# Heads of a gated DeltaNet: output norm as three columns through memory, triangular inverse handed on by tile in two PSUM banks

## The reference

```python
lmat = jnp.where(strict, jnp.einsum('nbhid,nbhjd->nbhij', k_beta, kb) * decay, 0.0)
sol = lax.linalg.triangular_solve(lmat + jnp.eye(c), rhs, left_side=True, lower=True, unit_diagonal=True)
...                                   # then a scan over chunks: v_new, o_c, state s
gate = jax.nn.silu(h @ w_g).reshape(bsz, t, GDN_HEADS, GDN_DV)
o = rmsnorm(o, o_norm_g) * gate       # o * rsqrt(mean(o*o over the 128 channels) + EPS) * g
return o.reshape(bsz, t, GDN_HEADS * GDN_DV) @ w_out, new_buf, s_new
```

## Time and profile before

| what | value |
|---|---|
| three runs, median | 1553.15 us (1552.4 to 1556.8) |
| the profiled execution | 1552.87 us, span 1551.2 us, granted clock 0.99 |
| TensorE busy | 1517.4 us, 98% of the span |
| VectorE, ScalarE, GpSimd busy | 52%, 47%, 70% |
| DMA | 212.47 MB, mean 137 GB/s |

### The profile page before, as it was taken

One profiled execution on the slowest core, in us unless ns is written; L12 is line 12 of the kernel. 1 busy time (PEld: TensorE's weight loads), 2 busy tenths in 40 slices (PEclk: granted clock), 3 DMA queues, 4 the chain that ended last, 5 costly groups with the idle time before them and its releaser, 6 DMA issues.

```text
span 1551.2 us, 32241 instructions
## 1 busy us (share of the span) xinstructions
PE 1517.4 (98%) x10218; PEld 1472.9 (95%) x10218; DVE 800.8 (52%) x1791; ACT 734.7 (47%) x1406; POOL 1081.6 (70%) x1040
## 2 busy tenths in 40 slices
PE   9999999999999999999999999999899999999998
PEld 8999999998999999888999999999888889999997
DVE  4555454017555413996655521576667776555401
ACT  6654444446444435556544433557544434443432
POOL 5568887774777678985867777666655656767674
PEclk9999999999999999999999999999999999999999
DMA  6334444552444655322565445544412225444353
GB/s 237 125 128 146 153 154 151 150 153 87 162 148 150 160 150 170 93 71 73 159 170 156 144 129 146 187 136 136 138 44 93 72 95 175 155 153 145 121 152 110
DMA packets 88109, 212.47 MB, mean 137 GB/s; under 512 B 25600, under 2 KB 33312, under 8 KB 88032
## 3 DMA queue, kind: packets, MB, share of 16 engines
q1 hardware_dynamic: 88032, 211.49, 42.7%
HBM read 201.80 MB, written 9.66 MB: 136 GB/s over the span
## 4 chain that ended last, share of the span: by engine, by line
PE 91%; DVE 5%; issue 1%; ACT 1%; POOL 1%; DMA 1%; DVEq 0%; SPq 0%; POOLq 0%; ACTq 0%
PE bank L887 26%; PE bank L889 26%; PE bank L888 26%; PE bank L1125 2%; PE bank L1264 1%; PE bank L1275 1%; PE bank L1319 1%; PE bank L1178 1%; POOL M L715 0%; DMA fst<-in_d_st 0%; DVE bank L2242 0%; PE bank L1349 0%; PE bank L1150 0%; DVE ssq L1934 0%; PE bank L1301 0%
## 5 line engine op out<-in xcount | busy, mean ns | idle before, releaser
L609 POOL TENSOR_TENSOR wlo<-raw,whi 128x512 fp32r<-128x512 f32 (+3 forms) x398 | 457.8, 1150 | 379.2 <-ACT whi L1412 341.5
L887 PE MATMUL bank<-Gh,whi 128*128 128x320 f32 x1912 | 596.4, 312 | 3.3 <-DVE M L2224 1.9
L889 PE MATMUL bank<-Gh,wlo 128*128 128x320 f32 x1912 | 590.9, 309 | 0.0
L888 PE MATMUL bank<-Gl,whi 128*128 128x320 f32 x1912 | 590.8, 309 | 0.0
L611 POOL TENSOR_TENSOR wlo<-raw,whi 128x512 fp32r<-128x512 f32 (+3 forms) x398 | 478.6, 1202 | 0.0
L1412 ACT ACTIVATE whi<-raw 128x1024 fp32r<-128x1024 f32 (+3 forms) x400 | 374.8, 954 | 51.5 <-PE bank L889 40.3
L887 PEld LDWEIGHTS bank<-Gh,whi 128*128 128x128 f32 x1912 | 359.0, 188 | 5.8 <-DVE M L2224 2.2
L888 PEld LDWEIGHTS bank<-Gl,whi 128*128 128x128 f32 x1912 | 359.0, 188 | 1.1
L889 PEld LDWEIGHTS bank<-Gh,wlo 128*128 128x128 f32 x1912 | 358.9, 188 | 0.0
L887 PE MATMUL bank<-Hh,whi 128*128 128x320 f32 x912 | 283.6, 311 | 4.0 <-DVE Hl L2183 2.5
L889 PE MATMUL bank<-Hh,wlo 128*128 128x320 f32 x912 | 281.8, 309 | 0.0
(11 more groups left out here) (389 smaller groups left out, 1807.1 us busy)
## 6 DMA issues: line engine op xcount, KB each, us to landing
raw<-in_f_up SPq DMA_DIRECT2D x176, 512.0 KB, 3.3
raw<-in_f_down SPq DMA_DIRECT2D x64, 384.0 KB, 3.1
raw<-in_f_down SPq DMA_DIRECT2D x64, 320.0 KB, 3.1
raw<-in_c_pw SPq DMA_DIRECT2D x24, 512.0 KB, 3.6
raw<-in_a_in SPq DMA_DIRECT2D x16, 512.0 KB, 4.2
raw<-in_d_qk SPq DMA_DIRECT2D x16, 512.0 KB, 3.6
raw<-in_d_vg SPq DMA_DIRECT2D x16, 512.0 KB, 3.5
raw<-in_a_out SPq DMA_DIRECT2D x8, 512.0 KB, 3.5
```

The lines of the kernel that those rows point to most:

```text
L609: pool.tensor_tensor(wlo[k][:, 0:half], raw[k][:, 0:half], whi[k][:, 0:half].bitcast(F32), ALU.subtract).then_inc(half_ready, 1)
L887: nc.tensor.matmul(dst, wh, h, start=start and n == 0, stop=False)
L888: nc.tensor.matmul(dst, wh, lo, start=False, stop=False)
L889: ins = nc.tensor.matmul(dst, wl, h, start=False, stop=stop and end and n == len(tiles) - 1)
```

## The change

It does two things. First, in levels 1 to 4 each product is written in two groups of tiles (`GROUPS`), each in its own bank, with a semaphore step per group: TensorE's product, ScalarE's copy and VectorE's subtraction of group 1 no longer wait for group 2. Level 0 stays one group of three; level 1 is split into tile 0 and tiles 1 and 2; levels 2 to 4 into two single tiles. The transposes still take a whole head. Second, the output norm's sums are three columns of 128 tokens (sq as the weight, one column of ones moving), ScalarE takes the root of the three columns of each head into `rinv`, VectorE takes one reciprocal of both heads' six columns at the start of the next pair, SyncE stores them to a DRAM row and loads the row back broadcast to all partitions into sq, and `head_scale` waits for that load. The decays of the queries (QT) move: head 0 before level 0, head 1 between level 0's subtractions and its transposes.

```diff
+        rinv = [dc[:, 2 + 3 * x:5 + 3 * x] for x in range(2)]
+        scr_r = nc.dram_tensor("scr_r", [HEADS, TW], F32).ap()
+        GROUPS = (((0, 3),), ((0, 1), (1, 3)), ((0, 1), (1, 2)), ((0, 1), (1, 2)), ((0, 1), (1, 2)))
+        COPIES, CHANGES = (2 * sum(len(g) for g in GROUPS[:n]) for n in (5, 4))
+        def group_at(lev, x):
+            return 2 * sum(len(g) for g in GROUPS[:lev]) + x * len(GROUPS[lev])
+        def below_bank(lev, g, x):
+            return bank[4 * x + (0, 1 if lev == 4 else 2)[g]]
+        def change_bank(g, x):
+            return bank[4 * x + (3, 1)[g]]
...
@@ SyncE @@
+            def gdn_norms(b):
+                sp.wait_ge(rinv_ready, b * 1 + 1)
+                for x in range(2):
...
+                        sp.dma_start(dst.rearrange("(i p) -> p i", p=P), rinv[x]).then_inc(norms_stored, 16)
+            def gdn_norm_loads(b):
+                sp.wait_ge(norms_stored, b * 32 + 32)
+                for x in range(2):
...
+                    sp.dma_start(sq[x][:, 0:NT], src.partition_broadcast(P)).then_inc(norms_in[x], 16)
...
                     with sp.Fori(1, 4) as b:
                         gdn_row_loads(b)
                         gdn_state_stores(b - 1)
+                        gdn_norms(b - 1)
                         gdn_state_loads(b)
+                        gdn_norm_loads(b - 1)
...
                     gdn_state_stores(3)
+                    gdn_norms(3)
+                    gdn_norm_loads(3)
...
@@ TensorE, below @@
-                        else:
-                            pe.wait_ge(tm_ready, b * 8 + (2 * (lev - 1) + x + 1))
+                        elif lev == 1:
+                            pe.wait_ge(kv_scaled, b * 2 + (x + 1))
                         pe.wait_ge(lv_ready, b * 10 + (2 * lev + x + 1))
-                        for c in range(3 if lev < 2 else 2):
-                            ins = nc.tensor.matmul(T(bank[4 * x], c), T(LV[x][lev], c), T(Tm[x], c), start=True, stop=True)
-                        ins.then_inc(lt_done, 1)
+                        for g, (a, z) in enumerate(GROUPS[lev]):
+                            if lev == 1:
+                                pe.wait_ge(tm_ready, b * CHANGES + (x + 1))
+                            elif lev > 1:
+                                pe.wait_ge(tm_ready, b * CHANGES + (group_at(lev - 1, x) + g + 1))
+                            for c in range(a, z):
+                                ins = nc.tensor.matmul(T(below_bank(lev, g, x), c), T(LV[x][lev], c), T(Tm[x], c),
+                                                       start=True, stop=True)
+                            ins.then_inc(lt_done, 1)
...
@@ TensorE, change @@
-                        pe.wait_ge(b_ready, b * 10 + (2 * lev + x + 1))
...
+                        if lev == 1:
+                            pe.wait_ge(qt_ready, b * 2 + (x + 1))
+                        for g, (a, z) in enumerate(GROUPS[lev]):
+                            pe.wait_ge(b_ready, b * COPIES + (group_at(lev, x) + g + 1))
+                            for c in range(a, z):
+                                ins = nc.tensor.matmul(T(change_bank(g, x), c), T(TT[x], c), T(Bm[x], c), start=True, stop=True)
+                            ins.then_inc(bt_done, 1)
...
@@ TensorE, last_change_turned @@
                         for c in range(2):
-                            ins = nc.tensor.matmul(T(bank[4 * x + 2], c), T(Bm[x], c), T(TT[x], c), start=True, stop=True)
-                        ins.then_inc(tb_done, 1)
+                            pe.wait_ge(b_ready, b * COPIES + (group_at(4, x) + c + 1))
+                            nc.tensor.matmul(T(bank[4 * x + 2 + c], c), T(Bm[x], c), T(TT[x], c), start=True, stop=True)\
+                                .then_inc(tb_done, 1)
...
@@ TensorE, sums of the output norm @@
-                        nc.tensor.matmul(bank[4 * x + 2][:, 0:NT], ones[:, :], sq[x][:, 0:NT], start=True, stop=True)\
-                            .then_inc(osum_done, 1)
+                        for i in range(3):
+                            ins = nc.tensor.matmul(bank[4 * x + 2][:, i:i + 1], sq[x][:, i * P:(i + 1) * P], ones[:, 0:1],
+                                                   start=True, stop=True)
+                        ins.then_inc(osum_done, 1)
...
@@ ScalarE @@
                         for x in range(2):
-                            act.wait_ge(lt_done, b * 10 + (2 * lev + x + 1))
-                            nc.scalar.activation(Bm[x][:, 0:w], bank[4 * x][:, 0:w], ACT.Copy).then_inc(b_ready, 1)
+                            for g, (a, z) in enumerate(GROUPS[lev]):
+                                act.wait_ge(lt_done, b * COPIES + (group_at(lev, x) + g + 1))
+                                nc.scalar.activation(Bm[x][:, a * P:z * P], below_bank(lev, g, x)[:, a * P:z * P],
+                                                     ACT.Copy).then_inc(b_ready, 1)
...
+                    nc.scalar.activation(spare1[:, 0:1], eps[:, 0:1], ACT.Sqrt)
                     for x in range(2):
                         act.wait_ge(osum_done, b * 2 + (x + 1))
-                        nc.scalar.activation(sq[x][:, 0:NT], bank[4 * x + 2][:, 0:NT], ACT.Sqrt, scale=1.0 / P,
+                        nc.scalar.activation(rinv[x], bank[4 * x + 2][:, 0:3], ACT.Sqrt, scale=1.0 / P,
                                              bias=eps[:, 0:1]).then_inc(osd_ready, 1)
...
@@ VectorE @@
+                def head_inverse(n):
+                    dve.wait_ge(osd_ready, n)
+                    vec.reciprocal(dc[:, 2:8], dc[:, 2:8]).then_inc(rinv_ready, 1)
...
+                def head_scale(b, x):
+                    dve.wait_ge(norms_in[x], b * 16 + 16)
+                    dve.wait_ge(og_ready, b * 2 + (x + 1))
                     vec.tensor_tensor(hbuf[x][:, :], hbuf[x][:, :], sq[x][:, 0:NT], ALU.mult).then_inc(h_mid, 1)
...
+                    if later:
+                        head_inverse(b * 2)
...
+                    queries_decayed(0)
                     for lev in range(5):
...
-                                dve.wait_ge(bt_done, b * 8 + (2 * lev + x + 1))
-                                vec.tensor_tensor(Tm[x][:, 0:w], Tm[x][:, 0:w], bank[4 * x + 3][:, 0:w], ALU.subtract)\
-                                    .then_inc(tm_ready, 1)
+                                for g, (a, z) in enumerate(GROUPS[lev]):
+                                    dve.wait_ge(bt_done, b * CHANGES + (group_at(lev, x) + g + 1))
+                                    vec.tensor_tensor(Tm[x][:, a * P:z * P], Tm[x][:, a * P:z * P],
+                                                      change_bank(g, x)[:, a * P:z * P], ALU.subtract).then_inc(tm_ready, 1)
+                            if lev == 0:
+                                queries_decayed(1)
...
-                            if later:
-                                head_invert(b * 2 - 2, lev // 2, 2 * (lev % 2))
-                                if lev >= 2:
-                                    head_invert(b * 2 - 2, lev - 2, 1)
...
                         if c == 0 and later:
-                            head_invert(b * 2 - 2, 0, 3)
-                            head_invert(b * 2 - 2, 1, 3)
-                            head_scale(b * 2 - 2, 0)
-                            head_scale(b * 2 - 2, 1)
+                            head_scale(b - 1, 0)
+                            head_scale(b - 1, 1)
...
-                for i in range(4):
-                    for x in range(2):
-                        head_invert(6, x, i)
+                head_inverse(8)
```

More of the change, by code:

```diff
@@ L478, in gdn_state_loads @@
                     sp.dma_start(SS[x], src).then_inc(states_in[x], 16)
+            def gdn_norms(b):
+                sp.wait_ge(rinv_ready, b * 1 + 1)
+                for x in range(2):
+                    h = b * 2 + x
+                    dst = scr_r[h, :] if isinstance(h, int) else scr_r[bass.ds(h, 1), :].rearrange("a n -> (a n)")
+                    with nc.allow_non_contiguous_dma(reason="three columns to a row"):
+                        sp.dma_start(dst.rearrange("(i p) -> p i", p=P), rinv[x]).then_inc(norms_stored, 16)
+            def gdn_norm_loads(b):
+                sp.wait_ge(norms_stored, b * 32 + 32)
+                for x in range(2):
+                    h = b * 2 + x
+                    src = scr_r[h, 0:NT] if isinstance(h, int) else scr_r[bass.ds(h, 1), 0:NT].rearrange("a n -> (a n)")
+                    sp.dma_start(sq[x][:, 0:NT], src.partition_broadcast(P)).then_inc(norms_in[x], 16)
             for name, l, n, w in phases:
@@ L1273, in change @@
                             pe.wait_ge(inv_ready, b * 10 + (2 * (lev - 1) + x + 1))
-                        for c in range(3 if lev < 2 else 2):
-                            ins = nc.tensor.matmul(T(bank[4 * x + 3], c), T(TT[x], c), T(Bm[x], c), start=True, stop=True)
-                        ins.then_inc(bt_done, 1)
+                        if lev == 1:
```

(24 more changed lines are left out.)

18 lines of the change are left out of this document (10 added, 8 removed).

## The result

The changed kernel takes **1587.21 us** (median of 4 runs, 1581.76 to 1592.22) against 1554.97 for the kernel before beside it: ratio 1.0198, 95% interval 1.0172 to 1.0223. Forecast were 1546.3, within 1542.8 to 1551.0. What happened is rival 3, the late store to memory, at a higher price than it was given. The profiled execution took 1592.22, with a span of 1590.5 against 1551.2.

The account below looks back on a forecast made before the run. The prediction took TensorE's stream to bound the kernel (91% of the chain). Terms 6.6+1.1-0.45-0.2-0.2 = 6.85 us off the profiled 1552.87 gave 1546.0, with the median 0.28 above: 1546.3 us, range 1542.8 to 1551.0.

Parts of the forecast that it names:

- rival 3: Norm store to memory lands late, holding row loads in pairs 1 and 2 and the tail: 1556.9 us; chance 0.07.
- the way through memory: SyncE's norm stores and loads back: landing taken as 3 us, hidden in pairs, costing 0.2 us in the last pair.
- rival 2: Half-clock stretches in pairs 1 and 2 go (-2.7 us), chunk 0 gives 0.5 more a pair: 1542.6; chance 0.13.
- Levels by tile: Inversion levels handing on 128-column tiles: gain 1.8 us in each of pairs 1 to 3, 1.2 in pair 0, sum 6.6.
- Reciprocals at chunk 0: Two reciprocals leave VectorE before head scaling: gain 0.7 us in pair 3, 0.2 each in pairs 1, 2; together 1.1.
- Columns: Norm sums as one-column matmuls: cost 0.45 us in the last pair, 0.2 in pair 0, hidden in pairs 1 and 2.

Follow-up runs that it names:

- apart: Changed kernel with each 4-byte norm element stored 512 bytes from its neighbour, the row loads reading another row (scaling wrong): 1555.02 us.
- apart64: Changed kernel with the 4-byte norm elements stored 64 bytes apart, scaling by the norms likewise wrong: 1553.00 us.
- rows: Changed kernel with the six norm columns turned into rows by TensorE, copied by ScalarE, stored as six 512-byte pieces: ratio 0.9991 to the kernel before.
- late: Changed kernel with the norm stores issued behind the state loads instead of ahead of them in pairs 1 to 3: 1581.03 us.
- no_memory: Changed kernel without the norm stores, the loads back and the wait for them (output scaled by leftover squares): ratio 0.9991 to the kernel before.
- tiles_only: Changed kernel with only the levels by tile, the output norm as in the kernel before: ratio 1.0002 to the kernel before.

## Why the prediction was wrong

**The failed step** is in the way through memory: "Its landing is not in the trace: from below 1.5, from above 7.4 ... I take 3, nearer to the lower end, since 1.5 KB is little data." Measured from the chain it is 10.2 to 11.7 us for the two stores, above even the upper bound. Bytes were the wrong measure. The 120-byte pieces of the earlier trace rows, at 6.0 to 7.4 us, were the nearest row in kind, and even their row was no bound, since it has no neighbours of 4 bytes. Apart landed in 1.7 us, apart64 in 2.0, and rows reached its norm load 1.2 to 3.2 us after the store. So the guess of 3 would have been about right, or too high, for each of the three other layouts tried. That the writes of neighbours into one piece of memory are done one after another is my reading; shown is only that adjacent addresses cost it and addresses 64 bytes apart don't. The Trainium skill, "DMA: Bandwidth & Descriptors" (Rules for kernel authors), advises against such an element-wise last dimension. The runs agree with the advice but not with its reason alone, since apart has as many single elements. The fixed 2 us per transfer of the same page of the Trainium skill (Latency and other measured facts) agrees with apart's 1.7 to 2.5 and not with this store's 10.2 to 11.7.

A second term failed with it. The sum has no term for a lower clock, and rival 2 prices "a further drop or two" at 1549, some 3 us. By the account below the clock took some 31 us of the profiled execution.

**Rival 3 had the right places, waits that were too long, and no clock.** Loss = 2(L-4.2)+(L-2.8): at L = 11 it gives 21.8, so 1568, not 1587. Its places are there. Relative to the first "below", the stores start 0.93 us ahead (forecast 1.1), the last row load is issued 14.45 behind (with L = 11 the forecast's sum gives 14.8), and the keys wait 5.27 us in pair 2 (forecast 6.8). TensorE lost 2.66 and 4.84 us to the keys, 7.5 together where the formula has 13.6. At the tail it gave 8.2, and the tail is 8.4 longer, but that agreement is luck. TensorE's waits there are 4.21+0.78 = 5.0 us, and it wanted tile 6 only 13.3 us after the first d_out product, where it was 10.8 before, because it ran partly at the lower clock. The norm load back was sized short too: 2.2 was taken, and the chain has 3.31. The formula left out three things:
- Levels. Pair 1 took 16.30 and pair 2 13.74 instead of 12.72. With the stores behind the state loads (late) this goes. In pair 1 TensorE waits 2.44 us for ScalarE's copies of level 2, and ScalarE itself stands 4.3 us for what the profile calls "remote". In pair 2 TensorE and VectorE stand 1.10 and 1.2 us with "issue". What reached them late stays open.
- State loads behind the stores: 13.0 us instead of 3.9. In pair 2 they had landed by 1233.7, and TensorE used them only after 1239.64, so it did not wait for them. Late shows that they alone don't carry the loss.
- The clock. Summed over the windows of all four pairs, some 66 us are at the lower level, against 13 before.

**How the loss divides.** Set against no_memory's profiled execution (span 1543.5 us), the changed kernel's span is 47.0 us longer. TensorE's six waits are 16.0 of it, and 31.0 are left. The changed kernel has 95 us at the lower level and no_memory 22. At 0.48 us each, the 73 us between them come to some 35, which covers the 31. This is an estimate, and too high where TensorE was waiting anyway. It holds stage by stage: pair 1's chunks should take 17.18+2.66+0.48x13.6 = 26.4 us and took 26.38, pair 2's 17.18+4.84+0.48x17.0 = 30.2 and took 30.22. The two long spells begin 2.3 and 0.1 us after TensorE resumes from the 2.66 and 4.84 us waits, with TensorE busy all through them (windows above). Waits are not the only thing before such spells, since apart has 51 us at the lower level without them. No run took the spells away with the waits left in.

**Levels by tile, 6.6 us.** The mechanism and nearly the size hold once memory is out: 12.72 a pair in no_memory against the forecast 12.5, below to below 1.96 against 2.1. Pair 0 reached 12.47 in tiles_only, and 13.27 in no_memory with a spell at the lower clock. In no_memory the levels gave 5.3 us in all. Counted for pairs 1 to 3 that is 1.6 each instead of 1.8. The split between its two causes was wrong: tiles alone gave 0.46, absent reciprocals alone 0.35, both 1.62. Either partner that is still late holds the level: that is my reading of why each half alone shows little. In the changed kernel itself pairs 2 and 3 still show part of it (13.74 against 14.34, 13.66 against 14.33).

**Reciprocals at chunk 0, 1.1 us.** Pair 3: 17.91 became 17.26 in no_memory, 0.65 against the 0.7 taken. Pairs 1 and 2: forecast 0.2 each, got 1.6 each, which is the spell at the lower clock that left the chunks (rival 2's event, priced there at 1.3). One of the two came back in the front of pair 2 (8.13 against 6.49), so half of it was shifted, not won. How much of the other half is lasting can't be read from one execution.

**Columns, -0.45 and -0.2.** From the norm sums to d_out 1.36 instead of 0.94, pair 0 1.36 instead of 1.18 (no_memory), and 1.63 in pairs 1 and 2, unchanged. All three as forecast.

**The profiled sum.** Without memory it would have been 1552.87-6.6-1.1+0.65 = 1545.8; no_memory's profiled execution took 1545.25. That it agrees so well is partly luck. The levels gave 5.3 and not 6.6, the chunks 3.9 and not 1.1, the fronts cost 1.7 that no term has, and 0.9 us had been won before the first "below", in code that is the same. Its median over ten runs was 1554.41, with a mean clock of 0.9864: a forecast from one execution at 0.990 had no term for the clock that the new kernel would draw. The range of 8.2 us was too narrow on that account too; the runs of before alone spread over 13.

**Chances.** 0.07 for rival 3, when its deciding point, 6.1 us, lay below the nearest landing of small pieces (median 6.4), was too low by the evidence on the table.

## What to carry to other kernels

Price a store by the addresses of its pieces, not by its bytes: single elements beside each other in memory took 8 to 12 us until the load behind the store could start, where the same elements 64 bytes apart, or turned into rows of 512 bytes first, took 1 to 4. Before a wait is put into a queue in order, list all that is queued behind it, and give the landing its full range there. Then ask what the wait does to the clock: here TensorE waited 16 us, and the lower clock, by estimate, cost some 31 more. If two partners are both late in a loop, try both repairs at once; and compare kernels at equal granted clock before a small gain is called none.

## What the runs showed of the hardware

- Two stores of 384 single 4-byte elements to adjacent addresses: 10.7 to 12.3 us from first issue to the dependent load, and 8.2 to 11.2 with the state loads ahead of them (late); one third of the elements: 8.2 to 10.7; all of them 512 or 64 bytes apart: landings of 1.7 to 2.9.
- While such a store is under way, 512 KB loads issued right behind it land in 13.0 us instead of 3.9, and the core's DMA moves 25 GB/s (228 in apart); issued right ahead of it, in 4.1.
- 3.4 us at the lower clock cost 1.6 us, in a front (6.49 to 8.13) as in the chunks (17.18 to 18.80).
- After waits of 2.66 and 4.84 us TensorE ran 13.6 and 17.0 us at a granted clock of 0.50 while busy throughout.
- The same kernel's times follow its mean granted clock: 0.001 is worth 1.0 to 1.5 us of 1550.
